# Layer starts on x times the gain, U and T of the triangular solve apart: a two-layer hybrid decoder step on one core

## The chip, the cores and the metric

The kernel runs on one core of a Trainium2 chip. The metric is the device time of one execution in microseconds, the median of the runs. Everything is float32 in memory.

## What is computed

264 tokens (256 of a prompt, 8 single steps with their own states) go through two layers of width 1024 and a last RMSNorm. Cut to what matters here:

```
for each layer:
  h  = RMSNorm(x, norm1)            # x * rsqrt(mean(x^2)) * gain
  p  = h @ W_in                     # GLU, q/k/v, z, a/b and gate columns
  yA = conv branch(p_glu)           # GLU, causal depthwise conv of 31 taps, LayerNorm, swish, W_out
  yB = gated delta rule(p_qkv, p_z, p_a, p_b)
       # conv(4), l2norm, per 128-token chunk:
       #   T = inverse(I + M), M strictly lower triangular; u = T v, w = T k; states
  x  = x + (sigmoid(gA) * yA + sigmoid(gB) * yB) @ W_o
  h2 = RMSNorm(x, norm2)
  x  = x + SwiGLU(h2)               # layer 0 dense (22 tiles of 128), layer 1 two of eight experts
```

## The kernel before

The data lie feature-major: xT and hT are 8 blocks of 128 features by 264 tokens. Weights come in tiles of 512 KB (1024 x 128) through a ring of six slots, loaded by SyncE in order; a slot is loaded again when its tile is used (load_static). Most tiles are multiplied as three products of split operands: ScalarE copies the tile to w_hi (high_part), VectorE subtracts to w_lo (low_part), and split_tile runs 24 matmuls of 264 columns, which for each feature block wait for x_lo. Four buffers hold split tiles. A few tiles (the set PLAIN: 0, 1 and 34 to 39) go as eight plain float32 matmuls straight from the ring. In this text a split tile and a plain tile are these two.

The order of work on each engine is written out by hand, with semaphores between the engines. A layer goes:

- model_squares on ScalarE, model_sums on TensorE (8 matmuls with a matrix of ones), model_rms (square root on ScalarE), reciprocal on VectorE, then hT = xT * gain * rstd, its copy x_hi and the rest x_lo.
- the a/b products (8 rows), plain tiles 0 and 1 (value and gate of the first GLU block), then split tiles 2 to 33. In between: the softplus chain for the decay on 12 columns, the convolutions of q/k/v (conv_qkv, two tiles at a time on VectorE), the l2 norm (rows_sum, square root, reciprocal, and twice `spread`, four matmuls with 8 rows that put a row on all partitions), Gram products.
- the inverse by doubling. For 8 units of 128 x 128 (2 chunks x 4 heads) units(3) holds T, units(4) its transpose U and units(7) M. After a start at level 0, levels v = 1 to 6 do on TensorE: B = M U (8 products), ScalarE copies B to units(8), one split tile, then T-side products for U and, except at the last level, for T. VectorE copies the masked blocks back into U and T and signals both with one semaphore, tu_done. Between these it runs the 31 taps of the depthwise convolution, in groups (conv_taps), and one low_part.
- transposes of k and v, three scalings of them, W, the chunk recurrence (v_new, out_and_state), 64 matmuls with two columns for the sample states, LayerNorm, merge, W_o (8 split tiles).

Layer 0 then has the FFN: sums and norm as above, 44 split tiles (gate and up alternating), and 8 output tiles of 22 plain matmuls (the down products), after which layer 1 starts with its sums. While W_o runs, GpSimd stores 12 blocks of zeros to memory (5.8 MB) that the routing of layer 1 needs. After layer 1 the expert stage runs split weight units to the end.

## Time and profile before

| | |
|---|---|
| median of 3 runs | 1646.61 us (1646.61 to 1647.78) |
| profiled execution | 1648.23 us, span 1646.4 us, mean granted clock 0.976 |
| TensorE busy | 1576.1 us (96%) |
| VectorE busy | 1209.6 us (73%) |
| ScalarE busy | 924.1 us (56%) |
| chain that ended last | TensorE 87%, VectorE 8%, ScalarE 3% |
| start of layer 0, FFN, layer 1, experts | 0, about 312, 533 and 847 us |

Busy time of TensorE counts matmuls that overlap, so 96% does not mean that it never waits. The start of each stretch is read from the timeline. Times of rows are from the start of the span; the profiled execution's own time is the span and 1.8 us around it.

### The profile page before, as it was taken

The numbers are of one execution on the slowest core, as the hardware profiler recorded it, in microseconds if no ns is written. First come the engines' busy times: TensorE is split into PE (matmuls) and PEld (weight loads), VectorE is DVE, ScalarE is ACT, GpSimd is POOL, SyncE is SP. The second block draws the span as 40 slices with busy tenths as digits, with TensorE's granted clock in tenths as the row PEclk, the third lists the DMA queues.
The fourth block names the chain that finished last, engine by engine and source line by source line (L and its number), as shares of the span: only waits on it lengthen the run. The fifth ranks groups of instructions, "written<-read, shape, count | busy, mean of one in ns | idle before, by whom it ended". The sixth has DMA issues, their size and how long they took to land.

```text
span 1646.4 us, 30478 instructions
## 1 busy us (share of the span) xinstructions
PE 1576.1 (96%) x10847; PEld 1415.7 (86%) x10847; DVE 1209.6 (73%) x1731; ACT 924.1 (56%) x1284; POOL 37.5 (2%) x52
## 2 busy tenths in 40 slices
PE   6998899899999898899989999999999999999997
PEld 4988886799988788897779899897989989798995
DVE  4776854554400687694559898999989899898987
ACT  4642151444300473233348778787777778777775
POOL 0000000200000000000003000000000000000000
PEclk9999889999999999989999999999999999999999
DMA  6551113865544553213459999999999999999993
GB/s 240 189 118 52 52 59 114 335 206 181 164 128 144 194 168 70 65 33 111 156 202 389 390 355 361 356 358 383 347 362 357 364 350 364 380 343 362 363 364 127
DMA packets 108893, 397.50 MB, mean 241 GB/s; under 512 B 13601, under 2 KB 13648, under 8 KB 108176
## 3 DMA queue, kind: packets, MB, share of 16 engines
q1 hardware_dynamic: 104464, 376.23, 64.7%
q0 software_dynamic: 4352, 20.20, 3.5%
q8 instruction: 53, 0.87, 0.2%
q14 instruction: 24, 0.20, 0.0%
HBM read 380.94 MB, written 16.43 MB: 241 GB/s over the span
## 4 chain that ended last, share of the span: by engine, by line
PE 87%; DVE 8%; ACT 3%; issue 1%; DMA 1%; SPq 0%; DVEq 0%; ACTq 0%
PE psum L1325 61%; PE psum L1591 5%; PE psum L1358 4%; PE psum L1536 2%; PE psum L1538 2%; DVE w_lo L835 2%; PE psum L1431 1%; PE psum L1495 1%; PE psum L1438 1%; DVE qkv L905 1%; PE psum L1442 1%; ACT w_hi L549 1%; DVE c L936 1%; PE psum L1545 1%; PE psum L1691 1%
## 5 line engine op out<-in xcount | busy, mean ns | idle before, releaser
L1325 PE MATMUL psum<-w_hi,h_hi 128*96 128x256 f32 x1408 | 399.7, 284 | 0.1
L1325 PE MATMUL psum<-w_hi,h_lo 128*96 128x256 f32 x1408 | 394.5, 280 | 0.0
L1325 PE MATMUL psum<-w_lo,h_hi 128*96 128x256 f32 x1408 | 393.7, 280 | 0.0
L1263 DVE TENSOR_TENSOR w_lo<-ring,w_hi 128x1024 fp32r<-128x1024 f32 x288 | 346.8, 1221 | 37.1 <-ACT w_hi L788 35.3
L788 ACT ACTIVATE w_hi<-ring 128x1024 fp32r<-128x1024 f32 x288 | 303.6, 1058 | 42.9 <-PE psum L1325 33.9
L1325 PE MATMUL psum<-hid_hi,w_hi 128*128 128x264 f32 x992 | 290.5, 293 | 8.1 <-DVE hid_lo L841 6.1
L1325 PE MATMUL psum<-hid_lo,w_hi 128*128 128x264 f32 x992 | 285.3, 288 | 0.0
L1325 PE MATMUL psum<-hid_hi,w_lo 128*128 128x264 f32 x992 | 285.0, 287 | 0.0
L1263 DVE TENSOR_TENSOR w_lo<-early,w_hi 128x1024 fp32r<-128x1024 f32 x192 | 231.3, 1221 | 18.2 <-ACT w_hi L788 18.1
L1325 PEld LDWEIGHTS psum<-w_hi,h_hi 128*96 128x96 f32 x1408 | 228.1, 162 | 0.8 <-DVE w_lo L1263 0.3
L1325 PEld LDWEIGHTS psum<-w_hi,h_lo 128*96 128x96 f32 x1408 | 228.5, 162 | 0.0
L1325 PEld LDWEIGHTS psum<-w_lo,h_hi 128*96 128x96 f32 x1408 | 227.7, 162 | 0.5
L788 ACT ACTIVATE w_hi<-early 128x1024 fp32r<-128x1024 f32 x192 | 202.3, 1058 | 35.0 <-PE psum L1325 30.0
L835 DVE TENSOR_TENSOR w_lo<-ring,w_hi 128x1024 fp32r<-128x1024 f32 x124 | 150.4, 1220 | 81.4 <-ACT w_hi L549 81.3
L549 ACT ACTIVATE w_hi<-ring 128x1024 fp32r<-128x1024 f32 x124 | 130.6, 1057 | 138.0 <-PE psum L1325 96.2
L1325 PEld LDWEIGHTS psum<-hid_hi,w_hi 128*128 128x128 f32 x992 | 190.8, 192 | 15.5 <-issue 10.7
L1325 PEld LDWEIGHTS psum<-hid_lo,w_hi 128*128 128x128 f32 x992 | 191.2, 193 | 0.1
L1325 PEld LDWEIGHTS psum<-hid_hi,w_lo 128*128 128x128 f32 x992 | 190.2, 192 | 0.0
L1325 PE MATMUL psum<-w_hi,hid_hi 128*96 128x512 f32 x352 | 139.8, 397 | 0.0
L1325 PE MATMUL psum<-w_hi,hid_lo 128*96 128x512 f32 x352 | 138.3, 393 | 0.0
L1325 PE MATMUL psum<-w_lo,hid_hi 128*96 128x512 f32 x352 | 137.9, 392 | 0.0
L936 DVE SCALAR_TENSOR_TENSOR c<-u_pad,prm,c 128x256 f32<-128x256 f32 x240 | 97.0, 478 | 0.0
(314 smaller groups left out, 1900.5 us busy)
## 6 DMA issues: line engine op xcount, KB each, us to landing
ring<-in_w_exp SPq DMA_DIRECT2D x288, 512.0 KB, 5.5
early<-in_w_exp SPq DMA_DIRECT2D x192, 512.0 KB, 5.5
ring<-in_w_mixer SPq DMA_DIRECT2D x112, 512.0 KB, 3.6
ring<-in_w_ffn SPq DMA_DIRECT2D x66, 512.0 KB, 3.7
qkv<-in_w_exp SPq DMA_DIRECT2D x48, 512.0 KB, 5.7
h_rows<-work POOLq DMA_DIRECT2D x12, 480.0 KB, 15.5
early<-in_s POOLq DMA_DIRECT2D x2, 2048.0 KB, 8.0
out_ss<-early POOLq DMA_DIRECT2D x2, 2048.0 KB, 9.5
```

What stands on the lines that cost most here:

```text
L549: A(w_hi[:, n % SPLIT, :], ring[:, p % RING, :, :].rearrange("p k n -> p (k n)"), ACT.Copy).then_inc(hi_done, 1)
L788: A(w_hi[:, buffer_x(u), :], slot_x(u % RING_X), ACT.Copy).then_inc(hi_done, 1)
L835: V.tensor_tensor(w_lo[:, n % SPLIT, :], ring[:, p % RING, :, :].rearrange("p k n -> p (k n)"), w_hi[:, n % SPLIT, :], ALU.subtract).then_ ...
L905: ins = V.scalar_tensor_tensor(qkv[:, t, 0:TP], q_pad[:, t, tap:tap + TP], w, qkv[:, t, 0:TP], ALU.mult, ALU.add)
L936: ins = V.scalar_tensor_tensor(c[:, j, 0:TP], u_pad[:, j, tap:tap + TP], w, c[:, j, 0:TP], ALU.mult, ALU.add)
L1263: V.tensor_tensor(w_lo[:, buffer_x(u), :], slot_x(u % RING_X), w_hi[:, buffer_x(u), :], ALU.subtract).then_inc(lo_done, 1)
L1325: last = M(out, lhs[x], rhs[w], start=(start and n == 0), stop=(stop and n == 2))
L1358: last = M(psum[:, i % 4, 0:T], w[:, k, :], hT[:, k, :], start=(k == 0), stop=(k == KD - 1))
L1431: last = M(pair(4)[:, u, :], units(7)[:, u, :], units(4)[:, u, :], start=True, stop=True)
L1536: M(psum[:, 2 * (t % 2), 0:T], w[:, j, :], c[:, j, :], start=(j == 0), stop=(j == CT - 1))
L1538: last = M(psum[:, 2 * (t % 2) + 1, 0:T], w[:, CT + h, :], qkv[:, 8 + h, :], start=(h == 0), stop=(h == H - 1))
L1591: last = M(psum[:, 6 + t % 2, 0:T], w[:, i % KD, :], act_all[:, f, :], start=(f == 0), stop=(f == FT - 1))
```

## The change

- x_gain = x times the norm's weight is made as soon as x is there (gain), in the first eight tiles of qkv, which are free then. The a/b products, tiles 0 and 1 of each layer, and the first gate and up tile of the FFN are multiplied with x_gain. rstd, the factor per token, is applied when their results leave PSUM: to the a/b rows, to the gate (before the sigmoid or silu) and to the value. hT for the split tiles is x_gain * rstd. The two FFN tiles become plain, so splitting starts with tile 2.
- The squares, sums and a/b products of layer 1 go into the last output tile of the FFN; half of the FFN's sums go in front of the last W_o tile.
- U and T have semaphores of their own (u_done, t_done), and the PSUM banks of the B and U products alternate from level to level. B waits for U, the T-side products for T.
- In the mixer: the square root of the l2 norm goes in front of the copy of tile 20, its reciprocal in front of that tile's low part; the last v convolution goes behind the first U; kv_taken counts twice; eight taps go behind the first copy of v_new. low_part(5) goes behind the softplus chain and glu(0) in front of it.
- x is loaded in two halves behind constants and parameters.

```diff
+        def b_bank(v):
+
+            return 4 if v % 2 else 6
+
+        def u_bank(v):
+            return 6 if v % 2 else 4
...
+        x_gain = qkv[:, 0:KD, :]
+        ab_row = work[0:2 * H, 7, 0:T]
...
-            sp.dma_start(xT[:, :, :].rearrange("p k t -> p (k t)"), a["xT"]).then_inc(x_loaded, 16)
             sp.dma_start(consts[:, :, :].rearrange("p k t -> p (k t)"), a["consts"]).then_inc(consts_loaded, 16)
             sp.dma_start(prm[:, :], a["params"]).then_inc(consts_loaded, 16)
+            for i in range(2):
+                sp.dma_start(xT[:, i * 4:i * 4 + 4, :].rearrange("p k t -> p (k t)"), a["xT"][:, i * 4 * T:(i + 1) * 4 * T]).then_inc(x_loaded[i], 16)
...
-                model_squares(2 * l)
                 if l == 0:
                     act.wait_ge(consts_loaded, 32)
-                for i in range(2, 2 + LEAD):
-                    high_part(section, i)
-                model_rms(2 * l)
+                    model_squares(0)
+                    model_rms(0)
+                    high_part(section, 2)
+                    high_part(section, 3)
+                else:
+                    model_squares(2, 0, 6)
+                    high_part(section, 2)
+                    model_squares(2, 6, 7)
+                    high_part(section, 3)
+                    model_squares(2, 7, 8)
+                    model_rms(2)
+                high_part(section, 4)
...
+                    if j == 0:
+                        act.wait_ge(gate_scaled, 2 * l + 1)
+                        A(glu_gate(0), glu_gate(0), ACT.Sigmoid).then_inc(glu_sig, 1)
+                        return
...
-                    A(units(8), pair(4), ACT.Copy).then_inc(b_taken, 1)
+                    A(units(8), pair(b_bank(v)), ACT.Copy).then_inc(b_taken, 1)
                     if v == 1:
                         z_silu(3)
+                        silu_qkv(5, 10)
...
-                model_squares(2 * l + 1)
+                if l:
+                    model_squares(3)
                 if l == 0:
-                    model_rms(2 * l + 1)
-
-                    high_part("ffn", 0)
+                    model_squares(1, 0, 6)
+                    high_part("ffn", 2)
+                    model_squares(1, 6, 8)
+                    model_rms(1)
+                    high_part("ffn", 3)
                     for k in range(KD):
                         act.wait_ge(h_done, KD + k + 1)
                         A(x_hi[:, k, :], hT[:, k, :], ACT.Copy).then_inc(x_hi_done, 1)
-                    for u in range(1, 2 * FT + 2):
+                    for u in range(4, 2 * FT + 2):
...
+            def gain(stage, k, g_name, g_at):
+
+                V.tensor_scalar(x_gain[:, k, :], xT[:, k, :], par(g_name, g_at + k), None, ALU.mult).then_inc(x_gain_done, 1)
+
+            def norm_parts(l2, split_stage):
+
+                for k in range(KD):
+                    V.tensor_tensor(hT[:, k, :], x_gain[:, k, :], rstd[:, :], ALU.mult).then_inc(h_done, 1)
+                    if k:
+                        x_low(split_stage, k - 1)
+                x_low(split_stage, KD - 1)
...
-                for k in range(KD):
-                    V.scalar_tensor_tensor(hT[:, k, :], xT[:, k, :], par("norm1", l * KD + k), rstd[:, :], ALU.mult, ALU.mult).then_inc(h_done, 1)
-                for k in range(KD):
-                    x_low(3 * l, k)
-
                 dve.wait_ge(ab_rows, l + 1)
-                V.tensor_copy(rstd[0:2 * H, :], psum[0:2 * H, 6, 0:T]).then_inc(ab_copied, 1)
-                for i in range(2, 2 + LEAD):
-                    low_part(section, i)
+                V.tensor_tensor(ab_row, psum[0:2 * H, 4, 0:T], rstd[0:2 * H, :], ALU.mult).then_inc(ab_copied, 1)
+                norm_parts(2 * l, 3 * l)
+                if l == 0:
+                    low_part(section, 2)
+                dve.wait_ge(units_used, base_ord[section] + 2)
+                if l:
+                    dve.wait_ge(zero_stored, 16 * (JOB_ROWS // ZERO_ROWS + 1))
+                V.tensor_tensor(glu_gate(0), psum[:, 1, 0:T], rstd[:, :], ALU.mult).then_inc(gate_scaled, 1)
...
-                    low_part(section, 22 + i)
-                    conv_qkv(4 + i, V_AT + 2 * i)
+                    if i == 0:
+                        low_part(section, 22)
+                conv_qkv(4, V_AT)
+                low_part(section, 23)
...
-                V.copy_predicated(units(3), mask_bits(level_masks, 0), units(7))
+                V.copy_predicated(units(3), mask_bits(level_masks, 0), units(7)).then_inc(t_done, 1)
                 dve.wait_ge(first_tr, l + 1)
-                V.copy_predicated(units(4), mask_bits(level_masks_t, 0), pair(4)).then_inc(tu_done, 1)
+                V.copy_predicated(units(4), mask_bits(level_masks_t, 0), pair(4)).then_inc(u_done, 1)
                 low_part(section, 25)
+                conv_qkv(5, V_AT + 2)
                 for v in range(1, LEVELS):
                     n_pq = (2 * (LEVELS - 1) - 1) * l + 2 * (v - 1)
                     conv_taps(2 * v - 1, 2 * v + 1)
                     dve.wait_ge(pq_mm, n_pq + 1)
-                    ins = V.copy_predicated(units(4), mask_bits(level_masks_t, v), pair(6))
+                    V.copy_predicated(units(4), mask_bits(level_masks_t, v), pair(u_bank(v))).then_inc(u_done, 1)
                     if v < LEVELS - 1:
                         dve.wait_ge(pq_mm, n_pq + 2)
-                        ins = V.copy_predicated(units(3), mask_bits(level_masks, v), pair(4))
-                    ins.then_inc(tu_done, 1)
+                        V.copy_predicated(units(3), mask_bits(level_masks, v), pair(b_bank(v))).then_inc(t_done, 1)
...
-                V.tensor_tensor(units(7), pair(4), bc(kdsc), ALU.mult)
+                V.tensor_tensor(units(7), pair(4), bc(kdsc), ALU.mult).then_inc(kv_taken, 1)
...
-                conv_taps(16, 18)
                 for cc in range(NC):
                     dve.wait_ge(vn_mm, NC * l + cc + 1)
                     V.tensor_copy(work[:, 2, cc * 512:cc * 512 + 512], psum[:, 6, :]).then_inc(vn_taken, 1)
                     if cc == 0:
-                        conv_taps(18, 19)
+                        conv_taps(16, 18)
...
+                    if l == 0:
+                        gain(1, t, "norm2", 0)
...
-                    dve.wait_ge(x_done, KD)
-                    low_part("ffn", 0)
-                    model_norm(1, "norm2", 0, hT, h_done, 2)
+                    low_part("ffn", 2)
+                    dve.wait_ge(rms_done, 2)
+                    settle(V.reciprocal(rstd[:, :], rstd[:, :]))
+                    norm_parts(1, 2)
 
                     dve.wait_ge(state_out, 16 * 4)
-                    for u in range(1, 2 * FT + 2):
+                    low_part("ffn", 3)
+                    dve.wait_ge(units_used, base_ord["ffn"] + 1)
+                    V.tensor_tensor(silu_g[:, 0, :], psum[:, 0, 0:T], rstd[:, :], ALU.mult).then_inc(gate_scaled, 1)
...
+                        dve.wait_ge(down_taken, t + 1)
+                        gain(2, t, "norm1", KD)
+                        if t >= 6:
+                            low_part("mix1", t - 4)
...
+            def ab_products(l, k0=0, k1=KD):
+
+                for k in range(k0, k1):
+                    pe.wait_ge(x_gain_done, 2 * KD * l + k + 1)
+                    last = M(psum[0:2 * H, 4, 0:T], par_block("w_ab", l, KD * 8)[:, k * 8:(k + 1) * 8], x_gain[:, k, :], start=(k == 0), stop=(k == KD - 1))
+                if k1 == KD:
+                    last.then_inc(ab_rows, 1)
...
+                project(0)
+                project(1)
+                pe.wait_ge(ab_copied, l + 1)
...
-                    pe.wait_ge(tu_done, LEVELS * l + v)
+                    pe.wait_ge(u_done, LEVELS * l + v)
                     for u in range(U):
-                        last = M(pair(4)[:, u, :], units(7)[:, u, :], units(4)[:, u, :], start=True, stop=True)
+                        last = M(pair(b_bank(v))[:, u, :], units(7)[:, u, :], units(4)[:, u, :], start=True, stop=True)
...
+                    pe.wait_ge(t_done, (LEVELS - 1) * l + v)
...
-                pe.wait_ge(kv_taken, l + 1)
+                pe.wait_ge(kv_taken, 2 * l + 1)
...
+                    if l == 0 and t == KD - 2:
+                        model_sums(1, 0, 4)
                 if l == 0:
-                    model_sums(1)
-
-                    for f in range(FT):
+                    model_sums(1, 4, KD)
+                    for i in range(2):
+                        w = arrived("ffn", i)
+                        for k in range(KD):
+                            pe.wait_ge(x_gain_done, KD + k + 1)
+                            last = M(psum[:, i, 0:T], w[:, k, :], x_gain[:, k, :], start=(k == 0), stop=(k == KD - 1))
+                        last.then_inc(units_used, 1)
+                    for f in range(1, FT):
...
+                        if f == FT - 1 and t >= 2:
+                            model_sums(2, t - 2, t - 1)
+                            ab_products(1, t - 2, t - 1)
+                    ab_products(1, KD - 2, KD - 1)
+                    model_sums(2, KD - 2, KD)
+                    ab_products(1, KD - 1, KD)
```

TensorE at the start of layer 0, before (L1338 the sums, L1367 the a/b products, L1358 a plain tile, L1372 the a/b rows turned by 128):

```order
L1338 MATMUL psum<-gs,consts 128x264 [waits squares_done] x8
L1367 MATMUL psum<-hT,prm 8x264 [waits h_done,masks_ready]
L1367 MATMUL psum<-hT,prm 8x264 [waits h_done] x7
L1358 MATMUL psum<-hT,ring 128x264 [waits slot_loaded0]
L1358 MATMUL psum<-hT,ring 128x264 x7
L1372 MATMUL psum<-consts,rstd 128x8 [waits ab_copied]
L1372 MATMUL psum<-consts,rstd 128x8 x2
```

The same place in the changed kernel (L1401 the sums, L1409 the a/b products, L1433 a plain tile):

```order
L1401 MATMUL psum<-gs,consts 128x264 [waits squares_done] x8
L1409 MATMUL psum<-qkv,prm 8x264 [waits x_gain_done] x8
L1433 MATMUL psum<-qkv,ring 128x264 [waits slot_loaded0]
L1433 MATMUL psum<-qkv,ring 128x264 x7
L1433 MATMUL psum<-qkv,ring 128x264 [waits slot_loaded1]
L1433 MATMUL psum<-qkv,ring 128x264 x7
L1442 MATMUL psum<-consts,work 128x8 [waits ab_copied]
```

The a/b products and both plain tiles now read qkv, where x_gain lies, and wait for x_gain_done and the weights only; the turn of the a/b rows (L1442) stands behind the plain tiles.

ScalarE at the start of the FFN, before (L549 the copy of a weight tile, L533 a square, L539 the square root):

```order
L549 ACTIVATE w_hi<-ring 128x1024 [waits units_used,slot_loaded0]
L549 ACTIVATE w_hi<-ring 128x1024 [waits units_used,slot_loaded1]
L533 ACTIVATE gs<-xT 128x264 [waits x_done,x_loaded]
L533 ACTIVATE gs<-xT 128x264 [waits x_done] x7
L555 ACT_TABLE_LOAD
L555 ACTIVATE small<-prm 128x1
L539 ACTIVATE rstd<-psum,prm 128x264 [waits sums_done]
```

The same place in the changed kernel (L562 the copy of a weight tile, L546 a square, L552 the square root):

```order
L562 ACTIVATE w_hi<-ring 128x1024 [waits units_used,slot_loaded0]
L562 ACTIVATE w_hi<-ring 128x1024 [waits units_used,slot_loaded1]
L546 ACTIVATE gs<-xT 128x264 [waits x_done] x6
L562 ACTIVATE w_hi<-ring 128x1024 [waits units_used,slot_loaded2]
L546 ACTIVATE gs<-xT 128x264 [waits x_done] x2
L568 ACT_TABLE_LOAD
L568 ACTIVATE small<-prm 128x1
L552 ACTIVATE rstd<-psum,prm 128x264 [waits sums_done]
```

The two copies ahead of the squares are of W_o tiles in both. The copy of FFN tile 2, which waits for its load into slot 2 of the ring, now stands between the squares.

VectorE at the first level, before (L835 the subtraction for a low part, L1016 and L1018 the first blocks of T and U, L936 taps of the depthwise convolution, L1024 and L1027 the blocks of U and T in a level):

```order
L835 TENSOR_TENSOR w_lo<-ring,w_hi 128x1024
L1016 COPY_PREDICATED work<-level_masks,work 128x1024
L1018 COPY_PREDICATED work<-level_masks_t,psum 128x1024
L835 TENSOR_TENSOR w_lo<-ring,w_hi 128x1024
L936 SCALAR_TENSOR_TENSOR c<-u_pad,prm,c 128x256 x8
L1024 COPY_PREDICATED work<-level_masks_t,psum 128x1024
L1027 COPY_PREDICATED work<-level_masks,psum 128x1024
```

The same place in the changed kernel (L865, L1068, L1070, L982, L1077 and L1080 are those lines now, L948 to L957 a q/k/v convolution):

```order
L865 TENSOR_TENSOR w_lo<-ring,w_hi 128x1024
L1068 COPY_PREDICATED work<-level_masks,work 128x1024
L1070 COPY_PREDICATED work<-level_masks_t,psum 128x1024
L865 TENSOR_TENSOR w_lo<-ring,w_hi 128x1024
L948 TENSOR_SCALAR qkv<-gs,prm 128x256 x2
L950 SCALAR_TENSOR_TENSOR qkv<-gs,prm,qkv 128x256 x2
L954 TENSOR_TENSOR rows<-gs,prm 128x64
L950 SCALAR_TENSOR_TENSOR qkv<-gs,prm,qkv 128x256 x4
L957 TENSOR_REDUCE qkv<-rows 128x2x8
L982 SCALAR_TENSOR_TENSOR c<-u_pad,prm,c 128x256 x8
L1077 COPY_PREDICATED work<-level_masks_t,psum 128x1024
L1080 COPY_PREDICATED work<-level_masks,psum 128x1024
```

The q/k/v convolution of the last v tiles (L948 to L957) now stands between the first U and the taps. The T copy is signalled apart from the U copy; that is not seen in rows without waits.

## Rows read from the trace of the kernel before

**Rows 1.** Two stretches: us, PE, PEld, DVE, ACT, POOL, clock, DMA, GB/s.

```profile
350.00:400.00 50.00, 50.00 (x416) 50.00 (x415) 24.31 (x26) 20.97 (x27) 0.00 (x0) 1.00 0.60 182
900.00:1646.00 746.00, 736.51 (x5286) 661.35 (x5284) 678.62 (x765) 579.00 (x693) 0.00 (x0) 1.00 0.94 350
```

**Rows 2.** TensorE to 36 us: start, us, line, tiles, count, idle before.

```profile
21.34 6.53 PE L1367 MATMUL psum<-hT,prm 128*8 128x264 f32 x16 [5.50 <-DVE hT L874]
27.81 3.83 PE L1358 MATMUL psum<-hT,ring 128*128 128x264 f32 x16
35.31 0.48 PE L1325 MATMUL psum<-hid_hi,w_hi 128*128 128x264 f32 x1
```

**Rows 3.** Timeline of VectorE, the first instruction.

```profile
9.53 0.23 DVE L860 TENSOR_SCALAR upper_bias<-consts 128x128 f32<-128x128 f32 x1 [9.53 <-DMA prm<-in_params]
```

**Rows 4.** Timelines of ScalarE and VectorE at the start of layer 0.

```profile
5.84 2.61 ACT L533 ACTIVATE gs<-xT 128x264 f32<-128x264 f32 x8 [3.83 <-DMA xT<-in_xT]
...
18.87 1.80 DVE L872 RECIPROCAL rstd<-rstd 128x264 f32<-128x264 f32 x1 [6.72 <-ACT rstd L539]
28.27 3.47 DVE L835 TENSOR_TENSOR w_lo<-ring,w_hi 128x1024 fp32r<-128x1024 f32 x3
```

**Rows 5.** Waits of TensorE, 84 to 250: line, releaser, total, times, longest.

```profile
PE psum L1431 <- DVE work L1027: 6.9, 5, 1.4
PE psum L1475 <- DVE work L1057: 2.3, 1, 2.3
PE psum L1431 <- DVE work L1018: 1.3, 1, 1.3
PE psum L1397 <- DVE rstd L1001: 0.9, 1, 0.9
PE psum L1457 <- DVE work L1040: 0.7, 1, 0.7
```

**Rows 6.** Timelines of the levels on TensorE and VectorE, and eight taps.

```profile
134.28 1.95 PE L1442 MATMUL psum<-work 128*128 128x128 f32 x16
...
124.58 1.31 DVE L1024 COPY_PREDICATED work<-level_masks_t,psum 128x1024 f32<-128x1024 int16 x1 [2.29 <-PE psum L1438]
...
134.49 1.30 DVE L1024 COPY_PREDICATED work<-level_masks_t,psum 128x1024 f32<-128x1024 int16 x1 [2.56 <-PE psum L1438]
...
189.42 3.25 DVE L936 SCALAR_TENSOR_TENSOR c<-u_pad,prm,c 128x256 f32<-128x256 f32 x8
```

**Rows 7.** Busy time and clock by stretch, two stretches at the lower clock.

```profile
102.00:105.00 3.00, 3.00 (x17) 3.00 (x15) 3.00 (x10) 0.00 (x0) 0.00 (x0) 0.53 0.87 81
194.00:214.00 20.00, 20.00 (x98) 20.00 (x97) 15.04 (x38) 3.81 (x13) 0.00 (x0) 0.51 0.01 1
```

**Rows 8.** TensorE: the second spread, the two-column products of both layers.

```profile
98.81 2.04 PE L1397 MATMUL psum<-rstd,consts 8*128 8x264 f32 x8
...
196.03 13.65 PE L1495 MATMUL psum<-qkv,early 128*128 128x2 f32 x64
...
716.20 10.54 PE L1495 MATMUL psum<-qkv,early 128*128 128x2 f32 x64
```

**Rows 9.** Start of the FFN: ScalarE, TensorE, issue of tile 2.

```profile
313.07 1.28 ACT L555 ACT_TABLE_LOAD   x1
315.73 0.48 ACT L539 ACTIVATE rstd<-psum,prm 128x264 f32<-128x264 f32 x1 [1.16 <-PE psum L1338]
...
321.78 0.56 PE L1325 MATMUL psum<-hid_hi,w_hi 128*128 128x264 f32 x1 [6.09 <-DVE hid_lo L841]
...
328.90 0.39 PE L1325 MATMUL psum<-hid_hi,w_hi 128*128 128x264 f32 x1 [1.17 <-DVE w_lo L835]
...
ring<-in_w_ffn SPq DMA_DIRECT2D x1, 512.0 KB, 10.9
```

**Rows 10.** Timeline of TensorE at the start of layer 1: sums, first split tile.

```profile
533.28 3.72 PE L1338 MATMUL psum<-gs,consts 128*128 128x264 f32 x16
...
554.86 0.48 PE L1325 MATMUL psum<-hid_hi,w_hi 128*128 128x264 f32 x1
```

104 lines of the change are left out of this document (59 added, 45 removed).

## The prediction

> **What bounds the kernel now.** I read the stretch table first. In a dense stretch of the FFN, TensorE runs 416 matmuls in 50 us at clock 1.00, so a weight tile of 24 products ("split tile") takes 2.9 us, and the expert stage from 900 us on has TensorE busy 736.5 of 746 us [rows 1]. Nothing in the change touches that stage: it can start earlier, not get shorter. What can be won lies ahead of 850 us, where TensorE stands still. The timeline of TensorE gives the start of layer 0: idle 5.50 us before the a/b products, those paced at the low clock (6.53 us for eight), two plain tiles, and the first split tile at 35.31 [rows 2]. The same picture stands in front of the FFN and of layer 1. The list of waits of TensorE between 84 and 250 us names six others, all for VectorE: five times 1.4 us per doubling level (6.9), then 2.3, 1.3, 0.9, 0.7 and, as the last of the list, 0.6 [rows 5]. The list of layer 1 has the same six, with 0.5 for the last. So the kernel is bound by TensorE's order of work, and its loss in front of the experts is waits for VectorE plus the low clock.
>
> **Start of layer 0.** Parameters landed at 9.53 [rows 3], x at 5.84 [rows 4]. Now constants and parameters go first and x in halves behind them; the bytes in front of the last one are the same, so the second half lands at about 9.5. Four squares (2.61 for eight [rows 4]) end at 10.8, the last sum at about 12.5 (11.3 if the eight sums run at 2.4 GHz, 14.2 at the low level). The a/b products follow at once (as the eight of a plain tile, 3.8 [rows 2]): 16.3. Then come the two plain tiles, which now read x times the gain and wait for no norm: 16.3 + 7.6 + 0.4 = 24.3. Beside them VectorE does the reciprocal (1.80 [rows 4]), scales the a/b rows (0.4, 16.8), makes eight normed blocks with their low parts at 0.74 each (eight steps of the first FFN tile: 327.73 - 321.78 [rows 9]) plus 0.5, 23.3, and the low part of tile 2 (3.47 for three [rows 4]): 24.5. The first split tile starts at about 24.6 instead of 35.31. I give back 0.6 for tile 5, whose low part now stands behind the softplus chain. Saved: 10.1 (8.3 to 11.5, from the two ends of the sums and a stall of 0 to 1).
>
> **The mixer, per layer.** 0.9: the square root goes ahead of a weight copy, the reciprocal ahead of a low part; gone. 0.6: the second normalising multiply no longer stands behind the q/k/v convolution; gone. 0.7: the W product waits for two of three scalings (1.2 each); gone. 2.3: eight conv taps (3.25 [rows 6]) move behind the copy that TensorE waits for; gone. 1.3: stays, since it hangs on the copy of weight tile 24, which waits for tile 21 on TensorE. The levels: the B product now waits for U alone. U's copy takes 1.30 and starts when the first of two products is done, beside the second (1.95) [rows 6], so it is hidden with 0.4 to spare; T's copy is needed only a split tile later. A level takes 9.9 now (U's copies start at 124.58 and 134.49) and would take 8.5; VectorE has 1.30 + 1.30 + 1.2 + 3.25 = 7.05 of work in it, so it keeps up. In the first level it has the moved convolution too (again eight operations of 0.4, 3.25). It stood idle for 2.29 before U's copy, so the copy starts 1.0 later, at 125.55, and ends 0.65 after the products: 6.9 - 0.65 = 6.25. Sum 0.9 + 0.6 + 0.7 + 2.3 + 6.25 = 10.7 in layer 0 and 10.6 in layer 1. Bounds: 4 less each, if three of the five level waits are only renamed; 1.3 more, if the fourth wait goes as well.
>
> **The clock in the mixer.** The granted clock is 0.53 at 102 to 105 us and 0.51 from 194 to 214 [rows 7], that is the lower of its two levels (1.2 GHz). The first of these follows the second spread, eight matmul records of 2.04 us with 8 of 128 rows, which had no idle time before it [rows 8]; a split tile there takes 4.5 instead of 2.9, and there are two such places per layer. The second stretch holds the 64 products with two columns: 13.65 us in layer 0, where the wait of 2.3 stood just before and the clock was down throughout; 10.54 in layer 1 [rows 8], so about half of them ran at the upper level. Without that wait I expect both layers to look like a better layer 1: 4 us off in layer 0, 1 in layer 1. The spreads keep their low rows and I expect half of their cost to stay: 1.5 saved per layer. Sum 8, between -2 and 17.
> [...]
>
> **Start of the FFN.** Four of the sums move in front of the last output tile, which moves 1.9 us of work and no more. But the copy of weight tile 2 now stands on ScalarE in front of squares 6 and 7, and that tile lands late: it is issued at about 305.5 and takes 10.9 us, because of the zero rows that are stored then [rows 9]. So: landing 316.4, copy 1.05, two squares 0.8: 318.3. Table load and root 1.28 + 0.2 + 0.48 [rows 9]: 320.3. Reciprocal 322.1, eight blocks 328.7, low part of tile 3: 330.0. TensorE meanwhile has a gap of 3 us behind its sums, ends them at 318.8, and does the two plain tiles until 326.4 and tile 2 behind the blocks until 329. Tile 3 starts at 330.0. Before, tile 1 started at 328.90 [rows 9] and tile 3 at 328.90 + 5.8 = 334.7. Saved 4.7; 8.3 if the copy does not delay the squares, 3 if the gap brings the clock down.
>
> **Start of layer 1.** Call T the end of the down products, 533.4 [rows 10]. The first split tile started at 554.86 and ended at T + 24.4. Now six sums and six a/b products (5.6 us) stand inside the last down tile. After it: add, square 1.0, load and root 2.0, reciprocal 1.8, a/b rows 0.4, blocks 6.5: the last at T + 11.7, and tile 2 ends at T + 12.1; the two plain tiles end at 9.6 and are hidden. 24.4 - 12.1 - 5.6 = 6.7. Tile 5's low part waits for the softplus chain (two table loads at 1.28 and a dozen short instructions) and costs 1.4. Saved 5.3 (4 to 7).
>
> **Sum.** 10.1 + 10.7 + 10.6 + 8 + 4.7 + 5.3 = 49.4. The profiled execution took 1648.23 (span 1646.4), so the same execution would take 1598.8; it lies 1.6 above the median of 1646.61, so I forecast 1597.
>
> **Rivals.**
> The clock stays up where the gaps go. For it: the 64 products took 10.54 in layer 1 and 13.65 in layer 0, so the clock there is not fixed. Against it: the second spread. It would bring the rest of the low clock back: four spreads at 1.5 (6), and 9 of what the 64 products and their neighbours lose in both layers, where VectorE's 36 taps (14.6 us at 3.25 for eight) become the limit: 6 + 9 = 15 instead of 8. Time 1590.
> The waits are only renamed. VectorE is busy 7.05 of 8.5 us in a level; if each level then waits for the copy of T, for ScalarE or for a late U, the levels give nothing (-12.5), and with a low clock at the FFN start and nothing from the clock (-8) the time is 1617. For it: each level's margin is 0.4 us. Against: T has a tile's time, and ScalarE does one weight copy and two evacuations in a level.
> The change does less than it says: the first tiles still wait, for instance because x lands much later behind the parameters. It would cost the 10 of the start: 1607. The row of x (landed at 5.84) speaks for some of it, the equal byte count against more.
> Slower than before: the clock falls in the levels. Place: the six levels of each layer, 128-column f32 products with one split tile in between, at 1.00 today despite 1.4 us of idle in 9.9. If the new order brought the lower level there, each us of TensorE work would cost one more: 2 x 6 x 8.5 = 102, and 1699. It decides from half of the levels on. Against it: less idle time, not more.
>
> **How the numbers follow.** Forecast 0.70 (its own range 1590 to 1605), clock stays up 0.10, waits renamed 0.11, start not gained 0.06, slower 0.03. The range 1588 to 1611 holds the first two, the third in part and the fourth. A measurement of this kernel can tell about 0.2%, 3.3 us: faster by more 0.96, within it 0.01, slower 0.03.
>
> **What would show it.** First split tile of layer 0 at 24 to 26 us. In the waits of TensorE only a wait for U in the first level, and one of 1.3 in front of it. A level of 8.5 us. On ScalarE at about 316 a wait for the DMA of FFN tile 2, with the last two squares behind it. Tile 3 of the FFN about 25 us earlier than 334.7. Expert stage of the same length. If the levels are still 9.9 us, or the expert stage changes by more than 3 us, I am wrong in substance.

## The result and the profile after

| | before | changed kernel |
|---|---|---|
| median | 1647.11 us (4 runs, 1646.61 to 1647.78) | 1624.50 us (4 runs, 1612.91 to 1634.62) |
| profiled execution | 1648.23 us, span 1646.4 | 1634.62 us, span 1632.8 |
| ratio | | 0.9866, 95% interval 0.9829 to 0.9904 |

The change makes the kernel faster by 22.6 us. I had forecast 49.6 less, at 1597, and a range up to 1611: wrong, 27 us of the forecast gain are not there. The four times also lie 22 us apart, where those of before lie within 1.2. So there are two questions: did the steps in front of the experts do what I said, and what else happened?

I first compared places that both traces have. "Saved" is the difference of their times.

| place on TensorE | before | after | saved so far | this stretch | forecast |
|---|---|---|---|---|---|
| first split tile of layer 0 | 35.31 | 28.16 | 7.2 | 7.2 | 10.1 |
| end of the 64 two-column products, layer 0 | 209.68 | 186.38 | 23.3 | 16.2 | 16.2 |
| ScalarE's weight copy behind the FFN's first split tiles | 335.06 | 309.64 | 25.4 | 2.1 | 4.7 |
| first split tile of layer 1 | 554.86 | 524.12 | 30.7 | 5.3 | 5.3 |
| end of the 64 products, layer 1 | 726.74 | 680.85 | 45.9 | 15.2 | 13.1 |
| first product of the experts' gather | 847.03 | 801.37 | 45.7 | -0.2 | 0 |
| end of the span | 1646.4 | 1632.8 | 13.6 | -32.1 | 0 |

(The forecast of a mixer is its waits, 10.7 or 10.6, and its share of the clock, 4 + 1.5 or 1 + 1.5.) In front of the experts 45.7 of 49.4 us are there. The expert stage, which no line of the change touches, gave 32.1 of them back. Two stretch rows show it (busy times of PE, PEld, DVE, ACT and POOL, the clock, the DMA share, GB/s); the one of before, from the gather on:

```profile
847.03:1646.40 799.37, 789.42 (x5712) 714.02 (x5712) 724.41 (x832) 618.58 (x743) 17.65 (x12) 0.99 0.94 347
```

and that of the changed kernel:

```profile
801.37:1632.80 831.43, 800.95 (x5712) 722.72 (x5712) 725.71 (x832) 619.62 (x743) 17.65 (x12) 0.97 0.91 335
```

The same 5712 matmul records take 831 us instead of 799, at a mean clock of 0.97. The waits of TensorE in that stage (total, times, longest) have one line that the list of before does not have at all:

```profile
PE psum L1388 <- issue: 20.5, 6, 3.8
PE psum L1713 <- DVE work L1272: 4.4, 1, 4.4
```

"issue" is time in which the engine waited for nothing that the profile shows. The timeline of TensorE at the first of three places, 1005, 1210 and 1414 us:

```profile
1005.15 0.52 PE L1388 MATMUL psum<-w_hi,h_hi 128*96 128x256 f32 x1 [2.87 <-issue]
1005.47 0.42 PE L1388 MATMUL psum<-w_lo,h_hi 128*96 128x256 f32 x1
1005.68 0.42 PE L1388 MATMUL psum<-w_hi,h_lo 128*96 128x256 f32 x1
1005.89 0.42 PE L1388 MATMUL psum<-w_hi,h_hi 128*96 128x256 f32 x1
1010.11 0.53 PE L1388 MATMUL psum<-w_lo,h_hi 128*96 128x256 f32 x1 [3.80 <-issue]
```

Four products, then another gap of 3.80 us. Such a pair stands at the other two places too (3.41 and 3.27, 3.63 and 3.54). Each place is the head of a pass of the loop over expert jobs, but only of every second pass. The trace names no engine that TensorE waited for; VectorE and ScalarE worked on through the first gap and then stood idle as well. What did differ is a line of the page on the queue that brings instructions (packets, MB, share). Before:

```profile
q8 instruction: 53, 0.87, 0.2%
```

After:

```profile
q8 instruction: 80, 1.31, 0.3%
```

27 packets more, of 16 KB each (1.31 MB / 80). In the kernel before this queue brought TensorE's program about once: its trace holds 22895 records of TensorE, or 13601 if six of the seven passes of the loop (1549 each) are counted out, and from packet to packet 257 to 258 of them go by in the mean, which makes 53 packets. Counted in windows of 4 us, nine of them fall into each pass that begins with a gap and none into the passes between. In the kernel before, only one packet moves between 1024 us and the last 20 us. So the code of the loop was fetched again, three times. The gaps are 20.5 of the 32 us; the clock accounts for most of the rest, as the windows of 1 us show it at its lower level from 1004.8 to 1015, 1210 to 1220 and 1415 to 1425 us. Stretch rows of the changed kernel, at three places of low clock:

```profile
180.00:190.00 10.00, 10.00 (x47) 10.00 (x48) 10.00 (x26) 3.10 (x11) 0.00 (x0) 0.50 0.00 1
296.00:301.00 5.00, 5.00 (x13) 3.82 (x12) 3.03 (x5) 3.21 (x6) 0.00 (x0) 0.50 0.89 359
1005.00:1010.00 5.00, 1.16 (x4) 0.82 (x4) 0.96 (x1) 0.00 (x0) 0.00 (x0) 0.50 0.79 295
```

The last one holds the second gap: the clock fell to its lower level (0.50) at the end of the first gap (0.84 from 1004 to 1005) and came back at 1015 us.

The rows that answer to those of before, in the order of the groups. Start of layer 0, ScalarE and then TensorE, for [rows 2 to 4]:

```profile
9.48 1.28 ACT L546 ACT_TABLE_LOAD   x1 [9.48 <-DMA xT<-in_xT]
10.77 2.61 ACT L546 ACTIVATE gs<-xT 128x264 f32<-128x264 f32 x8
...
11.25 5.58 PE L1401 MATMUL psum<-gs,consts 128*128 128x264 f32 x16 [4.11 <-ACT gs L546]
16.75 3.73 PE L1409 MATMUL psum<-qkv,prm 128*8 128x264 f32 x16
...
28.16 0.39 PE L1388 MATMUL psum<-hid_hi,w_hi 128*128 128x264 f32 x1
```

The first split tile stands at 28.16. ScalarE waited for x until 9.48 and only then loaded the table for the squares (1.28); in the kernel before it had done that at 0.73, under the load of x. The mixer's waits between 84 and 250 us, for [rows 5]:

```profile
PE psum L1503 <- DVE work L1070: 1.4, 1, 1.4
PE psum L1610 <- ACT gs L699: 0.5, 1, 0.5
PE psum L1503 <- DVE work L1077: 0.4, 1, 0.4
```

The wait on L1503 for L1070 is the 1.3 us that I left in; the one for L1077 is the late U of the first level, 0.4 instead of my 0.65. All else of [rows 5] is gone (the 0.5 for ScalarE was there before, too). VectorE's copies of U in the first two levels, for [rows 6]:

```profile
116.47 1.30 DVE L1077 COPY_PREDICATED work<-level_masks_t,psum 128x1024 f32<-128x1024 int16 x1
...
124.60 1.31 DVE L1077 COPY_PREDICATED work<-level_masks_t,psum 128x1024 f32<-128x1024 int16 x1 [1.37 <-PE psum L1511]
```

8.1 us apart; the B products of TensorE stand 8.3 us apart from the second level on, where I had 8.5. The 64 products, for [rows 8]:

```profile
175.56 10.82 PE L1569 MATMUL psum<-qkv,early 128*128 128x2 f32 x64
...
670.25 10.60 PE L1569 MATMUL psum<-qkv,early 128*128 128x2 f32 x64
```

The FFN's start, for [rows 9]:

```profile
293.89 1.06 ACT L562 ACTIVATE w_hi<-ring 128x1024 fp32r<-128x1024 f32 x1 [9.54 <-DMA ring<-in_w_ffn]
294.86 0.72 ACT L546 ACTIVATE gs<-xT 128x264 f32<-128x264 f32 x2
...
295.31 2.12 PE L1401 MATMUL psum<-gs,consts 128*128 128x264 f32 x4 [3.41 <-ACT gs L546]
```

ScalarE waits 9.54 us for the DMA of tile 2 with two squares queued behind the copy, and TensorE waits 3.41 us for them.

### The profile page after: what moved, and what is told of

The parts are those of the page before. It is cut to its first block, busy times and chain, and to the rows that moved or that the text cites. A ratio compares the mean times of both kernels' runs of the same rounds, so it can differ in the third digit from the quotient of the medians.

```text
span 1632.8 us, 30478 instructions
## 1 busy us (share of the span) xinstructions
PE 1577.3 (97%) x10831; PEld 1415.4 (87%) x10831; DVE 1215.7 (74%) x1759; ACT 925.5 (57%) x1284; POOL 37.7 (2%) x52
## 3 DMA queue, kind: packets, MB, share of 16 engines
q8 instruction: 80, 1.31, 0.3%
## 4 chain that ended last, share of the span: by engine, by line
PE 92%; DVE 5%; issue 1%; DMA 1%; ACT 1%; SPq 0%; DVEq 0%; ACTq 0%
PE psum L1388 66%; PE psum L1672 5%; PE psum L1433 3%; PE psum L1610 2%; PE psum L1612 2%; DVE c L982 2%; PE psum L1503 1%; PE psum L1511 1%; PE psum L1401 1%; PE psum L1619 1%; PE psum L1778 1%; PE psum L1515 1%; PE psum L1469 1%; DMA ring<-in_w_ffn 1%; PE psum L1569 1%
## 5 line engine op out<-in xcount | busy, mean ns | idle before, releaser
L1388 PE MATMUL psum<-w_hi,h_hi 128*96 128x256 f32 x1408 | 403.9, 287 | 10.0 <-issue 9.9
L1388 PE MATMUL psum<-w_lo,h_hi 128*96 128x256 f32 x1408 | 397.9, 283 | 10.6 <-issue 10.6
L1388 PE MATMUL psum<-hid_hi,w_hi 128*128 128x264 f32 x976 | 284.1, 291 | 0.9 <-DVE hT L1161 0.8
L1388 PE MATMUL psum<-hid_lo,w_hi 128*128 128x264 f32 x976 | 279.2, 286 | 0.0
L1388 PE MATMUL psum<-hid_hi,w_lo 128*128 128x264 f32 x976 | 278.9, 286 | 0.0
L1388 PEld LDWEIGHTS psum<-w_hi,h_hi 128*96 128x96 f32 x1408 | 231.5, 164 | 11.8 <-issue 11.3
L1388 PEld LDWEIGHTS psum<-w_lo,h_hi 128*96 128x96 f32 x1408 | 230.9, 164 | 11.9 <-issue 11.6
L562 ACT ACTIVATE w_hi<-ring 128x1024 fp32r<-128x1024 f32 x122 | 128.4, 1057 | 150.2 <-PE psum L1388 88.1
L865 DVE TENSOR_TENSOR w_lo<-ring,w_hi 128x1024 fp32r<-128x1024 f32 x122 | 147.9, 1218 | 75.3 <-ACT w_hi L562 75.1
L1388 PEld LDWEIGHTS psum<-hid_hi,w_hi 128*128 128x128 f32 x976 | 186.6, 191 | 7.9 <-issue 4.9
L1388 PEld LDWEIGHTS psum<-hid_lo,w_hi 128*128 128x128 f32 x976 | 186.7, 191 | 0.1
L1388 PEld LDWEIGHTS psum<-hid_hi,w_lo 128*128 128x128 f32 x976 | 185.7, 190 | 0.0
L982 DVE SCALAR_TENSOR_TENSOR c<-u_pad,prm,c 128x256 f32<-128x256 f32 x240 | 96.8, 480 | 0.0
```

The costliest lines, as they stand in the source:

```text
L562: A(w_hi[:, n % SPLIT, :], ring[:, p % RING, :, :].rearrange("p k n -> p (k n)"), ACT.Copy).then_inc(hi_done, 1)
L865: V.tensor_tensor(w_lo[:, n % SPLIT, :], ring[:, p % RING, :, :].rearrange("p k n -> p (k n)"), w_hi[:, n % SPLIT, :], ALU.subtract).then_ ...
L982: ins = V.scalar_tensor_tensor(c[:, j, 0:TP], u_pad[:, j, tap:tap + TP], w, c[:, j, 0:TP], ALU.mult, ALU.add)
L1388: last = M(out, lhs[x], rhs[w], start=(start and n == 0), stop=(stop and n == 2))
```

## Experiments

A word on the place of code. The packed trace also holds the instructions of TensorE that the page does not count as busy. In the straight code in front of the loop the packets of the instruction queue come 257 to 258 of these records apart in the mean (from the second packet to the 46th, 11342 records in 44 steps in the kernel before and 11309 in the changed kernel; single steps lie between 139 and 381). I take it as 256 instructions for a packet of 16 KB, which is an estimate from these counts; a piece below is 256 instructions in a row, and a boundary is where the next piece starts. The loop of the expert jobs on TensorE counts 1551 instructions in the compiled program, a little more than six pieces; the trace has 1549 records from one of its branches to the next. The first of these branches is TensorE's record 13485 in the changed kernel and 13507 in the kernel before: the change took 22 instructions away in front of it. The second gap came behind the loop's fourth weight load and product, twelve instructions into it (ten of them in the trace). If a boundary of the 256s lies there, the loop of the changed kernel reaches three instructions past a later boundary and touches eight pieces, and that of the kernel before touches seven. Places below are counted in instructions from the changed kernel's; by this count the loop touches eight pieces at the places -2 to 11, and seven at the others, all modulo 256. To move the loop, the kernels below have satisfied waits added on TensorE; two of them make one instruction (with 44 waits the page counts 30500 instructions instead of 30478, with 504 it counts 30730).

### The loop back on its old place, and the kernel before on the new one

```diff
 pe.wait_ge(consts_loaded, 32)
+for _ in range(44):
+    pe.wait_ge(consts_loaded, 32)
```

These are 22 instructions.

> The changed kernel with 22 instructions more on TensorE (satisfied waits, while it waits for the parameters at the start), so that its expert loop stands where it stood in the kernel before, counted from a multiple of 256 instructions. Theory A (the loop of 1551 instructions is cut by the boundaries of 256-instruction fetches, 16 KB each; at the place of the changed kernel it touches one piece more than stays loaded, so it is fetched again in every second pass): no issue gaps of TensorE in the expert stage, instruction packets back from 80 to about 53, and 1646.6 - 45.7 = 1601 us (1598 to 1604) with a spread of 1 us. Theory B (the expert stage starts 46 us earlier and its fetches meet other transfers): the gaps stay, 1613 to 1635 us, 80 packets. Theory C (the variation is of the chip and has nothing to do with the code's place): a spread over 10 us as before.

Measured: 1602.77 us (1601.66 to 1605.05), ratio 0.9729, interval 0.9713 to 0.9745. The page's line, and the expert stage:

```profile
q8 instruction: 53, 0.87, 0.2%
...
802.98:1603.20 800.22, 790.27 (x5712) 714.30 (x5712) 724.64 (x832) 618.91 (x743) 17.66 (x12) 0.99 0.94 347
```

53 packets, no gap, and the stage takes 800 us. Theory A gave 1601, and the spread fell from 22 to 3.4 us, where A had 1. B and C are out.

```diff
                 last.then_inc(sums_done, 1)
+                for _ in range(2 * 78 if l2 < 3 else 0):
+                    pe.wait_ge(consts_loaded, 32)
```

Three times 78, together 234 instructions (30712 on the page, 30478 before).

> The kernel before with 234 instructions more on TensorE (satisfied waits, 78 each behind three of the four sums, where TensorE waits for the norm anyway), so that its loop stands exactly where it stands in the changed kernel, modulo 256. Theory A: three pairs of issue gaps appear in the expert stage, 80 instruction packets instead of 53, time 1660 to 1680 us in the mean and a spread over 5 us. Theories B and C: 1647 us (up to 1650 if the waits show), 53 or 54 packets, no gaps.

Measured: 1674.46 us (1669.98 to 1687.49), ratio 1.0157, interval 1.0139 to 1.0176. The page's line and the waits in the expert stage:

```profile
q8 instruction: 90, 1.47, 0.4%
...
PE psum L1325 <- issue: 26.1, 8, 3.7
PE psum L1628 <- DVE work L1209: 4.4, 1, 4.4
```

The kernel before, with nothing changed in its work, gets the gaps (8 here, four pairs, where I had expected three), 37 packets more, and loses 28 us. Four times nine of them are the refetches, and one is left for the added instructions. From the gather on (847.85) its profiled execution lasts 38.4 us longer than that of before: 9.6 for each refetch.

### Where the edges are

The same edit with 16 and 28 waits, one execution each:

> Theory A in its sharp form: the gap came behind four weight loads and products of the loop, so the boundary lies 12 instructions behind the loop's start and 3 instructions in front of its end. With 8 instructions more the loop still crosses two boundaries too many: issue gaps of 15 to 22 us in the expert stage and about 80 instruction packets. Theories B and C: as the changed kernel too, so it tells only the size of the step.

Measured: 1615.46 us. The page's line and the gaps:

```profile
q8 instruction: 71, 1.16, 0.3%
...
PE psum L1388 <- issue: 14.6, 2, 7.9
```

Twice nine packets more, and two gaps, one for each refetch this time, of 14.6 us together; I had expected about 80 packets and 15 to 22 us. That the pair became one gap fits the count: here the boundary lies four instructions behind the loop's start, in front of its first product. From its gather (794.37) on the kernel takes 819.2 us, 9.5 for each refetch.

> Theory A in its sharp form: with 14 instructions more the loop's start has passed the boundary, so the gaps are gone, about 53 instruction packets, 1601 us. Theories B and C: gaps, 80 packets, 1613 to 1635 us.

Measured: 1604.53 us, and the page's line:

```profile
q8 instruction: 53, 0.87, 0.2%
```

The other edge, with the waits in front of the expert jobs, where TensorE idles for 4.4 us (252 instructions; 255, from 510 waits, in the second kernel; one execution each):

```diff
+for _ in range(504):
+    pe.wait_ge(consts_loaded, 32)
 pe.wait_ge(h_tok_done, 3)
 gather(0, 0)
```

> The other edge. 252 satisfied waits on TensorE in front of the expert jobs place the loop 4 instructions ahead of its place in the changed kernel, modulo 256. If the loop of 1551 instructions may touch seven pieces of 256 and not eight, and the boundary is where the second gap stood (behind the loop's twelfth instruction, so that its last three lie in the eighth piece), four instructions less take the last three out of it: no issue gaps, 53 or 54 instruction packets. The waits themselves cost about 0.11 us each, 20 to 28 us, so the time tells nothing. Rival 'only the loop's head near a boundary matters': gaps and 63 packets or more.

Measured: 1621.86 us, with a page line and one wait that is the added instructions themselves:

```profile
q8 instruction: 54, 0.88, 0.2%
...
PE psum L1713 <- issue: 26.4, 1, 26.4
```

> The same with 255, one instruction ahead of the place in the changed kernel: two of the loop's instructions lie in the eighth piece, so gaps of TensorE in the expert stage and 63 to 90 instruction packets. If there are none, the edge is not where this count puts it.

Measured: 1652.37 us.

```profile
q8 instruction: 81, 1.33, 0.3%
...
PE psum L1713 <- issue: 26.8, 1, 26.8
PE psum L1388 <- issue: 19.5, 6, 4.0
```

54 against 81 packets, no gap against six in the loop, 30 us apart, from three instructions. Both edges, and before_plus234 at the place 0 again after 256, are consistent with the count: the loop is fetched again at the places -1, 0 and 8, and stays loaded at -4, 14 and 22. The places between are not tried, so each edge is known to a few instructions only.

### U and T for themselves

All kernels from here on carry as many added waits as bring their loop to the place of after_plus22, and are compared with its 1602.8. All six have 53 packets and no gap in the loop.

```diff
+                    pe.wait_ge(t_done, (LEVELS - 1) * l + v)
                     pe.wait_ge(u_done, LEVELS * l + v)
```

> The changed kernel with its loop on the good place (22 instructions further, as in all the following ones) and B made to wait for T's copy too, as before the change; the alternating banks stay. Against 1602.8 us. Theory 'the level waits were real': 5 waits of 1.4 us in each layer come back, less what VectorE's work had left of them (0.65), so +12 us (10 to 14), 1615. Rival 'the waits are only renamed': 0 to +4.

Measured: 1619.05 us (1617.25 to 1619.84), ratio 0.9835, interval 0.9819 to 0.9851: 16.3 more. The wait is back with its price:

```profile
PE psum L1506 <- DVE work L1080: 14.0, 10, 1.5
```

Ten waits, 14.0 us; the two waits for the late U (0.7 in the changed kernel) are in them. The rival, that waits are only renamed, is out. But 16.3 is more than the 10 to 14 that I had expected, and more than the waits; what the rest is, is not settled. The clock of the spreads in layer 0 works the other way: it stayed at 1.00 from 86 to 98 us here, and was 0.72 in after_plus22.

### The taps in front of the v_new copy

```diff
                 low_part(section, 33)
+                conv_taps(16, 18)
...
-                    if cc == 0:
-                        conv_taps(16, 18)
-                    else:
+                    if cc:
                         conv_taps(27, 29)
```

> The eight conv taps go in front of the first copy of v_new again. Theory: the wait of 2.3 us comes back in both layers (+4.6), and with it a longer stretch at the lower clock in layer 0 (+0 to +3): 1607 to 1610. Rival 'something else was late behind it': +1 or less.

Measured: 1609.55 us (1607.24 to 1616.01), ratio 0.9771, interval 0.9755 to 0.9787: 6.8 more. The wait, and the two-column products of both layers behind it:

```profile
PE psum L1549 <- DVE work L1109: 6.4, 2, 3.2
...
181.11 13.65 PE L1570 MATMUL psum<-qkv,early 128*128 128x2 f32 x64
...
681.62 10.68 PE L1570 MATMUL psum<-qkv,early 128*128 128x2 f32 x64
```

The wait is 3.2 us in each layer, more than the 2.3 of [rows 5]. With it the products of layer 0 take 13.65 us again, to the digit of [rows 8], against 10.7 without (after_plus22): the lower clock is on from 176 to 201 us, and from 178 to 193 without the wait. In layer 1 they take 10.7 with the wait and 10.8 without. So the wait drew the clock term behind it in layer 0, as forecast, and not in layer 1. This profiled execution was the slowest of its four (1616.0; the others took 1607 to 1611), so its clock is not that of the median.

### The FFN's start

```diff
-                    model_squares(1, 0, 6)
-                    high_part("ffn", 2)
-                    model_squares(1, 6, 8)
+                    model_squares(1)
                     model_rms(1)
+                    high_part("ffn", 2)
...
-                    low_part("ffn", 2)
                     dve.wait_ge(rms_done, 2)
                     settle(V.reciprocal(rstd[:, :], rstd[:, :]))
+                    low_part("ffn", 2)
```

> The copy and the low part of FFN tile 2 go behind the square root and the reciprocal. The trace of the changed kernel has ScalarE waiting 9.5 us for the DMA of that tile with two squares queued behind, TensorE idle for 3.4 us and the lower clock until 302 us. Theory 'the queue order made the gap': the gap goes, the first FFN tiles run at the upper clock, and the blocks of the norm set the end: -4 us (-2 to -7), 1599. Rival 'the norm's chain is the bound anyway': 0 to -1.

Measured: 1597.84 us (1593.93 to 1599.03), ratio 0.9700, interval 0.9683 to 0.9717: 4.9 less. TensorE, last sums, the two plain tiles and the first split tile:

```profile
288.78 1.50 PE L1400 MATMUL psum<-gs,consts 128*128 128x264 f32 x6
290.11 7.28 PE L1656 MATMUL psum<-qkv,ring 128*128 128x264 f32 x32
297.04 0.48 PE L1387 MATMUL psum<-hid_hi,w_hi 128*128 128x264 f32 x1
```

No idle time and 7.28 us for the plain tiles, the upper clock. The queue order made the gap. How much the gap costs hangs on the clock: in after_plus8, which has the old order, TensorE waited 3.0 us there, the clock stayed at 1.00 from 295 to 302 us, and the gather came at 794.37, no later than the 795.24 of this kernel.

### x ahead of the constants

```diff
+            for i in range(2):
+                sp.dma_start(xT[:, i * 4:i * 4 + 4, :].rearrange("p k t -> p (k t)"), a["xT"][:, i * 4 * T:(i + 1) * 4 * T]).then_inc(x_loaded[i], 16)
             sp.dma_start(consts[:, :, :].rearrange("p k t -> p (k t)"), a["consts"]).then_inc(consts_loaded, 16)
             sp.dma_start(prm[:, :], a["params"]).then_inc(consts_loaded, 16)
-            for i in range(2):
...
-                    act.wait_ge(consts_loaded, 32)
                     model_squares(0)
+                    act.wait_ge(consts_loaded, 32)
```

> The two halves of x are loaded ahead of constants and parameters again (and the squares wait for x alone). Theory 'the start came 3.5 us later than forecast (28.2 against 24.6) because the squares with their table load began only at 9.5 us': the squares are done when the constants land, the sums end 2.5 us earlier, -2.5 us (-1.5 to -4), 1600. Rival 'the blocks of the norm and the weights' halves bound the start': 0.

Measured: 1600.91 us (1600.49 to 1605.15). The run is inconclusive: now the parameters land last, and the 22 added instructions stood right behind them.

```profile
11.83 0.91 PE L1419 MATMUL psum<-ident_bf,level_masks 128*128 128x128 bf16 x7 [11.83 <-issue]
12.53 5.16 PE L1401 MATMUL psum<-gs,consts 128*128 128x264 f32 x16
```

The first products came at 11.83 and not at 9.5. I moved the waits in front of the expert jobs:

> x ahead of the constants as in x_first, but the 22 satisfied waits stand where TensorE idles 4.4 us in front of the expert jobs instead of at the start. In x_first the first products of TensorE came at 11.83 us, 2.5 us behind the parameters (9.31), which the 22 waits had taken. Theory 'the waits hid the gain': first products at about 9.5, sums from 10.3 at TensorE's own pace, first split tile at 26 to 26.5 instead of 29.0: 1600 us (1598 to 1601.5), 2.5 below the 1602.8 of the changed kernel on the good place. Rival 'the start does not carry to the end': 1602 to 1603.

Measured: 1600.93 us (1599.66 to 1601.41), ratio 0.9719, interval 0.9704 to 0.9734. TensorE at the start:

```profile
9.84 0.91 PE L1417 MATMUL psum<-ident_bf,level_masks 128*128 128x128 bf16 x7 [9.84 <-DVE ident_bf L903]
10.54 5.98 PE L1401 MATMUL psum<-gs,consts 128*128 128x264 f32 x16
16.45 3.73 PE L1409 MATMUL psum<-qkv,prm 128*8 128x264 f32 x16
...
27.87 0.39 PE L1388 MATMUL psum<-hid_hi,w_hi 128*128 128x264 f32 x1
```

Sums started at 10.54, near the 10.3 expected, but took 5.98 us (5.58 in the changed kernel; 5.10 in the kernel before, whose squares had ended at 8.45), where sixteen records of a plain tile take 3.7. Stretch rows show their pace, first of x_first_b:

```profile
12.00:13.00 1.00, 1.00 (x4) 0.79 (x3) 0.44 (x2) 0.00 (x0) 0.00 (x0) 1.00 1.03 410
16.00:17.00 1.00, 1.00 (x6) 0.38 (x5) 0.00 (x0) 0.44 (x2) 0.41 (x2) 1.00 0.22 86
```

and then of the kernel before, in its a/b products at the lower clock:

```profile
22.00:23.00 1.00, 1.00 (x3) 0.28 (x2) 1.00 (x4) 1.00 (x4) 0.00 (x0) 0.50 0.95 410
```

Until 15 us TensorE did three or four records of 264 columns in a microsecond, as at the lower clock; from 15 us on six. So the sums ran at the pace of the lower level. The clock column reads 1.00 there, but the trace of x_first_b has no clock record before 15.0 us, so the column tells nothing of that stretch. An earlier start of the sums only moved more of them into that stretch. The first split tile came at 27.87, 0.3 earlier than in the changed kernel, not 2. The median is where I expected it, 1.8 below 1602.8, but not by the way that I had named, and the two intervals overlap: no gain is shown.

> x_first_b and ffn2_behind together. If the two gains (2.5 and 5) add up: 1595 us (1592 to 1597). If one hides the other (a transfer of the weights that sets the pace of both): 1598.

Measured: 1599.66 us in the median of five (1593.25 to 1599.83), ratio 0.9702, interval 0.9685 to 0.9718. That is ffn2_behind again, and 4.7 above the 1595 for two gains that add up. The lowest median of this study is that of ffn2_behind on the good place, 1597.8 us against 1624.5 of the changed kernel and 1646 of the one before. Its own times lie 5 us apart, those of `both` 6.6. One cause can be seen between the profiled executions: the lower clock followed all four spreads in `both` (85 to 89, 91 to 96, 576 to 580 and 583 to 587 us), and one of four in ffn2_behind (580 to 585). That this also makes the difference between the executions of one kernel is not shown; they have no traces, but the fastest of each had the highest mean clock (0.988 and 0.989).

## Why the prediction was wrong

**Step by step.**

- "Nothing in the change touches that stage: it can start earlier, not get shorter", and "Expert stage of the same length": this is the step that failed, a term that I put at nothing. The stage lasted 32.1 us longer in the profiled execution, and I had written that more than 3 would mean that I am wrong in substance. I had asked whether the change touches the work of the stage, and not whether it moves its code. Twenty-two instructions fewer in front of the loop put its end, by the count above, three instructions past a boundary. Each refetch cost 10.7 us there (32.1 / 3): two gaps, 6.8 (20.5 / 3), and the lower clock, on for 10.2 us each time, with 6 to 7 us of work at half speed in it, about 3. In the other kernels it was 9.3 to 9.6 (9.3 is that of after_plus255: its stage lasts 827.6 us, that of after_plus252 799.6). The number of refetches differed between kernels, two to four. The other three executions of the changed kernel have no traces: 1612.9, 1619.0 and 1630.0 us lie 10.1, 16.2 and 27.2 above 1602.8, which would suit one, one or two, and three refetches. That the spread of 22 us comes from their number is likely, since it fell to 3.4 without them, but it is not counted. The way to the gather varies too, by the clock: with the same work but for 14 of the added waits it came at 802.98 in after_plus22 and at 794.37 in after_plus8, where windows of 1 us show the lower clock for about 44 and 28 us.
- None of my rivals had it. "Slower" was put into the levels, which kept their clock.
- Start of layer 0, forecast 10.1, measured 7.2. The sums ended at 16.8 and not at 12.5. One part is the table load of 1.28 us, which the late x uncovers. Another is that x landed later than the equal byte count gave: VectorE waited until 9.5 for the first half and until 11.03 for the second, which I had at 9.5. The largest is the pace of the sums: I let the last of them end 1.7 us behind the squares, where the same sums had taken 5.10 us in the trace of before with all squares done; even my bound for the lower clock, 14.2, was too low. The runs show no clock in GHz, they show a pace: at the clock of 0.50 split products of 264 columns start 0.220 us apart in the median (kernel before) and those of 256 columns 0.213 (changed kernel), 1.2 columns in a ns; at 1.00 those of 264 columns start 0.121 us apart, 2.2 columns in a ns. The 1.2 and 2.4 GHz of the prediction are the first of these paces and its double, if one column takes one cycle; the runs show no more of them than that.
- Mixer of layer 0, forecast 16.2 with the clock, measured 16.2; layer 1 13.1 and 15.2. The waits went as listed, and ut_together and taps_back gave back 16.3 and 6.8 us when they were undone. That layer 0 agrees to the digit is partly luck. By windows of 1 us up to the end of the 64 products the lower clock lasted 22.5 us before and 14.2 after in layer 0, 17.3 and 10.8 in layer 1; half of the difference, 4.1 and 3.3, is an estimate of what the clock gave back (forecast 5.5 and 2.5), and the rest, 12.1 and 11.9, of what the waits and the shorter levels gave (10.7 and 10.6). The 64 products themselves gave 2.8 and nothing, where I had 4 and 1. The spreads are not fixed: in layer 0 the lower clock followed both (86 to 90 and 93 to 97 us), in layer 1 one of the two, and in ut_together, after_plus8 and ffn2_behind none of layer 0, with the same records of 2.04 us.
- FFN start, forecast 4.7, measured 2.1. The mechanism was right (the copy of tile 2 delays the last squares, with 9.54 us of wait for its DMA) and the branch for it was written: 3 "if the gap brings the clock down". It did (0.50 from 296 to 301 us). The zero rows beside the weights are in the trace of before: from 305 to 317 us GpSimd's queue moved 2.40 MB and the weights' queue 2.03, and a weight tile took 11.0 us to land in the median, against 4.6 from 330 to 345, where GpSimd's queue moved nothing.
- Start of layer 1, forecast 5.3, measured 5.3.

With the loop on its old place the same kernel takes 1602.8 us, 5.8 above my figure and inside my range. In its profiled execution the gather starts at 802.98, so 44.1 us are saved in front of it instead of 49.4, and the stage behind lasts 800.2 us against 799.4. These 5.3 and 0.8 are its distance from the forecast.

What stays loaded is shown for this one loop only: it stayed loaded where by the count it touches seven pieces, and was fetched again, though not in every pass, where it touches eight (53 packets in after_plus22, 80 in the changed kernel). In the straight code of this kernel TensorE has no wait that ends with "issue", other than those of the added instructions; at the loop's heads a refetch cost 9.3 to 10.7 us.

The lower clock came with the gaps of 3 to 4 us: it was on from 1005 to 1015 us (0.50), and it came with the FFN's 3.4 us gap too (0.50 from 296 to 301), though not with the one of 3.0 us in after_plus8 (1.00 from 295 to 302). With it a refetch cost more than its gaps, 10.7 us against 6.8.

## What to carry to other kernels

A change in front of a loop can move the loop's code, here by 22 instructions. The loop, 1551 instructions in seven or eight pieces of about 256, was fast or slow by its place alone, and three instructions more decided over 30 us. Read the instruction queue's packets and the waits that end with "issue" before believing that an untouched stage keeps its length and when its times suddenly spread. And in a hand-written order, nothing that waits for a DMA belongs in front of something short that another engine waits for: here two squares stood behind such a wait of 9.54 us, and TensorE was idle for 3.41.

## What the runs showed of the hardware

- A loop of 1551 instructions on TensorE took its six branches back with one packet in all when it touched seven pieces of 256 instructions by the count (the kernel before, after_plus22), and was fetched again (nine packets of 16 KB) at two to four of them when it touched eight. Why not at all six is open: in the changed kernel every second pass was spared, in before_plus234 two refetches came in passes that follow each other (1052 and 1161 us).
- A refetch showed as two gaps of 2.6 to 4.0 us, or as one of 6.7 or 7.9 (after_plus8), in a stage where the DMA engines were 91 to 94% busy with weights.
- A satisfied wait instruction on TensorE took about 0.11 us: 26.4 / 252 = 0.105 in after_plus252, where they ran beside the wait of 4.4, and (11.83 - 9.31) / 22 = 0.115 in x_first, from the landing of the parameters.
- A wait of 3.2 us ahead of the two-column products lengthened them from 10.7 to 13.65 us in layer 0 (taps_back), where the lower clock was on from 176 to 201 us (0.52) instead of from 178 to 193 (0.54), and not at all in layer 1.
- The same eight records with 8 of 128 rows (2.04 us, no idle time) were followed by the lower clock in some executions and not in others: the mean clock from 86 to 98 us was 0.72 in after_plus22 and 1.00 in ut_together.
- At the start of the program the first matmuls of 264 columns ran at three or four records per us up to 13 us in the kernel before and up to 15 us in x_first_b, the pace of the lower clock. The traces have no clock record before 13.4 and 15.0 us; the column's 1.00 there is not a measured one.
